# Gate rows fetched by transfers, half-chunk score products in couples of 64 rows, and three small moves in a two-layer decoder trunk

## The chip, the cores and the metric

The kernel runs on one core of a Trainium2 chip. The metric is the device time of one execution in microseconds, lower is better. Before the change it is 1235.92 us, the median of three runs (1235.68 to 1236.24). All times below are microseconds unless they are marked ns.

## The reference

Two decoder layers over 512 tokens of width 1024, in float32. Layer 0 mixes tokens with an mLSTM (4 heads of width 192, a matrix memory with input and forget gates), layer 1 with differential attention (6 pairs of heads of width 64). Both have a cross attention to 256 memory tokens and a SwiGLU block.

```python
def mlstm_mixer(h, w_in, conv_w, conv_b, gate_b, head_norm):
    p = h @ w_in
    qk_raw = p[..., :2 * MIX_WIDTH]                 # 2 * 768 columns
    gates = p[..., 4 * MIX_WIDTH:4 * MIX_WIDTH + 2 * M_HEADS] + gate_b
    qk = jax.nn.silu(causal_depthwise_conv(qk_raw, conv_w, conv_b))
    q = qk[..., :MIX_WIDTH].reshape(B, S, M_HEADS, M_HEAD_DIM)      # 4 heads of 192
    k = qk[..., MIX_WIDTH:].reshape(B, S, M_HEADS, M_HEAD_DIM) * (M_HEAD_DIM ** -0.5)
    i_pre, f_pre = gates[..., :M_HEADS], gates[..., M_HEADS:]
    hs = mlstm_chunkwise(q, k, v, i_pre, f_pre)     # scores q k^T, weighted by gate sums, causal
    ...

for i in range(DEPTH):                              # DEPTH = 2
    h = rmsnorm(x, norm1[i])
    mix, xq = mlstm_mixer(...) if i == 0 else diff_attention(...)
    xo = memory_cross_attention(xq, mem, mem_norm[i], w_mem_kv[i], xq_norm[i], xk_norm[i])
    x = x + concat([mix, xo]) @ w_out[i]
    h = rmsnorm(x, norm2[i])
    x = x + (silu(gate) * up) @ w_down[i]
```

## The kernel before, in words

Activations stand transposed: features on the partitions, the 512 tokens along the free axis, in eight tiles of 128 features. A **dense product** of a 128-wide output tile is a sum over eight input tiles `k`, and each `k` has three matmuls, because every operand is split into a rounded part and a rest (`Hh` and `Hl` for the input, `w_hi` and `w_lo` for the weight): `Hh,w_hi`, `Hl,w_hi` and `Hh,w_lo`, all of them in the fp32r type in one pass. SyncE (SP) loads one raw weight tile after another, GpSimd (POOL) splits each into `w_hi` (one instruction, L568) and `w_lo` (mostly one instruction per group of 256 columns, L573). Matmuls on plain f32 operands (`tmp,cn`, `QK`, `QK,KZ`, `rm,ones`) are run in two passes, and the trace has a record for each pass. The order of the work on each engine is written out by hand; engines wait for each other on semaphores.

**Start (0 to 140 us).** Projection tiles of layer 0 alternate with memory tiles (256 memory tokens, `Ah,w_hi` with 256 columns) and small jobs. The eight gate rows of the mixer (`i_pre`, `f_pre` for four heads) and eight lower parts of them come out of one product with 16 rows, `PS[0:16, 6]`; VectorE (DVE) scales them into `tmp[6][0:16]` (L1136, semaphore `g_free`). TensorE (PE) then adds upper and lower parts, and moves the result to partitions 0 to 3, with two selection products of 16 rows (L1658, L1659). The first sum goes to bank 6 (input gates) and is read by DVE when it forms `a_row`; the second goes to bank 3 (forget gates) and is read by ScalarE (ACT) at L699. Behind them on PE come the column sum of the memory's squares (`rm,ones`) and the first memory tile (`Ah,w_hi`).

**mLSTM scores (141 to 215 us).** A head is 192 wide, which is one full chunk of 128 features and half a chunk. Chunks 1 and 4 of q and of k (`HALF_CHUNK`) hold the halves of two heads each, in partitions 0 to 63 and 64 to 127. `head_scores(h)` forms four key blocks `s` of 128 keys; block `s` has `512 - 128 s` columns and its own bank of PSUM (`S_BANK`). Each block is two products over 128 rows: one on the full chunk, one on the half chunk, where the other head's 64 rows of k are zero. For that DVE writes zeros at L1141 and L1142 (semaphore `k_zero`), and `silu` (L657) puts the two halves of k of such a chunk in two instructions, one into `KZ`, one into `QK`. Blocks 0 and 1 wait until ACT has read the cross attention's scores from the banks (`ms_exp`), blocks 2 and 3 wait for `hout`, the two head-output instructions L1261 and L1262 of DVE. DVE weights each block when it is done (L1230, semaphore `s_done`).

**Differential attention (646 to 840 us).** Six pairs of heads, `c` = 0 to 5, are worked in turn among dense tiles. For pair `c` and query block `u`: PE forms the scores (`b_s`, matmuls named `QT_HI` and `QR_LO`), DVE masks them and takes the row maximum (`b_max`, L1453 to L1456), ACT takes exponentials (`b_exp`, L931, two activations each with a sum that is read out), DVE scales and subtracts (`b_prob`, L1465 to L1467), PE transposes (`b_t`, L1952, after ACT has emptied the bank by `b_at`, L940), and a product with V follows. The output `x` of an earlier pair is rounded meanwhile into the dense operand by ACT (`c_hi`, `Ah`, L986) and DVE (`c_lo`, `Al`, L1493), and `co_ready` tells PE.

## Time and profile before

| | us |
|---|---|
| median of three runs | 1235.92 |
| the profiled execution, its own time | 1235.87 |
| its span, first to last instruction | 1234.0 |
| PE busy | 1227.9 (99%) |
| POOL busy | 844.9 (68%) |
| DVE busy | 519.2 (42%) |
| ACT busy | 360.7 (29%) |

The profiled execution lies 1.9 us above its span, and within 0.1 us of the median. Busy time is the union of the records of an engine. [...] A record that spans several passes is marked by its count (x2, x4), and then runs from the first start to the last end.

### The profile page before, as it was taken

The numbers are of one execution on the slowest core, as the hardware profiler recorded it, in microseconds if no ns is written. First come the engines' busy times: TensorE is split into PE (matmuls) and PEld (weight loads), VectorE is DVE, ScalarE is ACT, GpSimd is POOL, SyncE is SP. The second block draws the span as 40 slices with busy tenths as digits, with TensorE's granted clock in tenths as the row PEclk, the third lists the DMA queues.
The fourth block names the chain that finished last, engine by engine and source line by source line (L and its number), as shares of the span: only waits on it lengthen the run. The fifth ranks groups of instructions, "written<-read, shape, count | busy, mean of one in ns | idle before, by whom it ended". The sixth has DMA issues, their size and how long they took to land.

```text
span 1234.0 us, 16220 instructions
## 1 busy us (share of the span) xinstructions
PE 1227.9 (99%) x5848; PEld 1002.9 (81%) x5848; DVE 519.2 (42%) x795; ACT 360.7 (29%) x716; POOL 844.9 (68%) x1029
## 2 busy tenths in 40 slices
PE   9999999999999999999999999999999999999998
PEld 7888877788888888888888777778888888888887
DVE  6954434644222233112345888884423113221331
ACT  6523456633220011001141666655322001100110
POOL 7998433567777777777776444536678777777775
PEclk9999999999999999999999999999999999999999
DMA  7234211123232222222243222222323223323223
GB/s 274 96 122 146 69 53 46 57 86 99 97 102 95 92 102 91 96 102 98 77 132 101 71 69 71 70 69 68 101 86 102 103 85 102 102 87 101 96 72 105
DMA packets 35067, 116.99 MB, mean 95 GB/s; under 512 B 4417, under 2 KB 4930, under 8 KB 34886
## 3 DMA queue, kind: packets, MB, share of 16 engines
q1 hardware_dynamic: 33416, 112.82, 27.4%
...
## 4 chain that ended last, share of the span: by engine, by line
PE 97%; DVE 1%; ACT 1%; issue 0%; DMA 0%; POOL 0%; ACTq 0%; SPq 0%; POOLq 0%
PE PS L1551 95%; PE PS L1952 1%; DVE nmB L1455 0%; DVE Al L1279 0%; PE PS L1795 0%; DMA w_raw<-in_wt_dram 0%; PE PS L1980 0%; PE PS L1921 0%; PE PS L1913 0%; PE PS L1619 0%; PE PS L1905 0%; DVE PS L1453 0%; DVE PB L1467 0%; ACT tmp L800 0%; ACT tmp L808 0%
## 5 line engine op out<-in xcount | busy, mean ns | idle before, releaser
L573 POOL TENSOR_TENSOR w_lo<-w_raw,w_hi 128x256 fp32r<-128x256 f32 (+1 forms) x800 | 617.5, 803 | 17.0
L568 POOL TENSOR_SCALAR w_hi<-w_raw 128x1024 fp32r<-128x1024 f32 (+2 forms) x204 | 214.7, 1052 | 356.8 <-PE PS L1551 356.7
L1551 PE MATMUL PS<-Hh,w_hi 128*128 128x512 f32 x1072 | 428.2, 399 | 0.0
L1551 PE MATMUL PS<-Hl,w_hi 128*128 128x512 f32 x1072 | 417.9, 390 | 0.3 <-DVE Hl L1059 0.3
L1551 PE MATMUL PS<-Hh,w_lo 128*128 128x512 f32 x1072 | 418.0, 390 | 0.0
L1551 PEld LDWEIGHTS PS<-Hh,w_hi 128*128 128x128 f32 x1072 | 201.3, 188 | 47.7 <-issue 8.1
L1551 PEld LDWEIGHTS PS<-Hh,w_lo 128*128 128x128 f32 x1072 | 201.2, 188 | 42.9
L1551 PEld LDWEIGHTS PS<-Hl,w_hi 128*128 128x128 f32 x1072 | 201.5, 188 | 40.4 <-issue 1.0
L1551 PE MATMUL PS<-Ah,w_hi 128*128 128x512 f32 (+1 forms) x544 | 207.9, 382 | 0.1
L1551 PE MATMUL PS<-Ah,w_lo 128*128 128x512 f32 (+1 forms) x544 | 205.0, 377 | 0.0
L1551 PE MATMUL PS<-Al,w_hi 128*128 128x512 f32 (+1 forms) x544 | 204.9, 377 | 0.0
L864 ACT ACTIVATE tmp<-tmp 128x512 f32<-128x512 f32 x44 | 27.9, 634 | 315.3 <-DVE tmp L1371 315.3
L1551 PEld LDWEIGHTS PS<-Ah,w_hi 128*128 128x128 f32 x544 | 102.3, 188 | 20.8 <-issue 1.5
L1551 PEld LDWEIGHTS PS<-Ah,w_lo 128*128 128x128 f32 x544 | 102.3, 188 | 19.0
L1551 PEld LDWEIGHTS PS<-Al,w_hi 128*128 128x128 f32 x544 | 102.4, 188 | 18.8 <-issue 0.5
L1373 DVE TENSOR_TENSOR tmp<-PS,rinv 128x512 f32<-128x512 f32 x44 | 30.4, 691 | 200.4 <-PE PS L1551 200.4
L866 ACT ACTIVATE Ah<-tmp 128x512 f32 x44 | 27.8, 632 | 251.7 <-DVE tmp L1376 251.7
L1371 DVE TENSOR_TENSOR tmp<-PS,rinv 128x512 f32<-128x512 f32 x44 | 30.4, 692 | 90.0 <-PE PS L1551 89.5
L1392 DVE TENSOR_TENSOR xT<-xT,PS 128x512 f32 x24 | 16.5, 688 | 105.8 <-PE PS L1551 105.8
L1334 DVE TENSOR_TENSOR xT<-xT,PS 128x512 f32<-128x512 f32 x40 | 27.4, 686 | 77.8 <-PE PS L1551 77.8
L1379 DVE TENSOR_TENSOR Al<-tmp,Ah 128x512 f32 x44 | 41.0, 931 | 40.0 <-ACT Ah L866 40.0
L1376 DVE TENSOR_TENSOR tmp<-tmp 128x512 f32<-128x512 f32 x44 | 39.3, 892 | 5.4
...
## 6 DMA issues: line engine op xcount, KB each, us to landing
...
QKR<-QKP ACTq DMA_DIRECT2D x24, 128.0 KB, 4.3
...
```

The lines of the kernel that those rows point to most:

```text
L568: nc.gpsimd.tensor_scalar(w_hi[:, sl, 0:nk], w_raw[:, raw, 0:nk], 0.0, 1.0, ALU.add, ALU.mult).then_inc(w_round, 1)
L573: lo = nc.gpsimd.tensor_tensor(w_lo[:, sl, w], w_raw[:, raw, w], w_hi[:, sl, w].bitcast(F32), ALU.subtract)
L864: nc.scalar.activation(tmp[0][:, 0:SEQ], tmp[1][:, 0:SEQ], ACT.Silu).then_inc(silu_done, 1)
L866: nc.scalar.activation(Ah[:, bass.ds(i, 1)], tmp[3][:, 0:SEQ].rearrange("p (a n) -> p a n", a=1), ACT.Copy).then_inc(f_hi, 1)
L1334: nc.vector.tensor_tensor(xT[:, k], xT[:, k], PS[:, bank], ALU.add).then_inc(dense_free, 1)
L1371: nc.vector.tensor_tensor(tmp[1][:, 0:SEQ], PS[:, base % 2], rinv[:], ALU.mult).then_inc(dense_free, 1)
L1373: nc.vector.tensor_tensor(tmp[2][:, 0:SEQ], PS[:, (base + 1) % 2], rinv[:], ALU.mult).then_inc(dense_free, 1)
L1376: nc.vector.tensor_tensor(tmp[3][:, 0:SEQ], tmp[0][:, 0:SEQ], tmp[2][:, 0:SEQ], ALU.mult).then_inc(gu_ready, 1)
L1379: nc.vector.tensor_tensor(Al[:, bass.ds(i, 1)], one, Ah[:, bass.ds(i, 1)].bitcast(F32), ALU.subtract).then_inc(f_ready, 1)
L1392: nc.vector.tensor_tensor(xk_, xk_, PS[:, b:b + 1], ALU.add).then_inc(dense_free, 1)
L1551: return nc.tensor.matmul(out_, a, b, start=start, stop=stop)
L1952: last = nc.tensor.transpose(PS[:, 2 + u % 2, k * P:(k + 1) * P], PB[:, 0, W_OFF[u] + k * P:W_OFF[u] + (k + 1) * P], ident)
```

## The change

Three parts. **Gates:** the two selection products on PE are gone. ACT issues three transfers inside SBUF, after `first_tap(0)`, which copy rows 4 to 7, 8 to 11 and 12 to 15 of `tmp[6]` to partitions 0 to 3 of `tmp[0]`, `tmp[7]` and `tmp[1]`; DVE adds upper and lower parts with two additions behind `mem_lo(0)`. **Half chunks:** `KZ` and the zeros go. SP issues eight transfers that put chunks 1 and 4 of q and k into `QSW` and `KSW` with their 64-row halves exchanged, four ahead of the load of tile `T_HEAD + 1`, four ahead of that of tile `T_HEAD + 5` (these wait for the fourth `s_done`). `head_scores` takes the key blocks two at a time: full chunk of the first, full chunk of the second, then both half chunks as products over 64 rows, the first on the head's own rows and the second on the exchanged copy, which lies in the other 64 rows of the array. **Attention:** `b_s(c, 3)` is issued one or two steps later in the dense tile, in the last pair too; `b_t(c, 1)` one step later; `c_hi` stands ahead of `b_exp(c, 2)`, `c_lo` ahead of `b_max(c, 3)`.

```diff
@@ SP, ahead of the load of tile n
+                if n in (T_HEAD + 1, T_HEAD + 5):
+                    i = (n - T_HEAD) // 4
+                    c = HALF_CHUNK[i]
+                    sp.wait_ge(qk_ready, MC + c + 1)
+                    if i:
+                        sp.wait_ge(s_done, NT)
+                    for r in (0, 64):
+                        sp.dma_start(QSW[64 - r:P - r, i], QK[r:r + 64, c]).then_inc(sw_in, 16)
+                        sp.dma_start(KSW[64 - r:P - r, i], QK[r:r + 64, MC + c]).then_inc(sw_in, 16)
                 load(n)
@@ ACT
-                if c - MC in HALF_CHUNK:
-                    act.wait_ge(k_zero, 1)
-                    nc.scalar.activation(KZ[64:P, HALF_CHUNK.index(c - MC)], y[64:P], ACT.Silu)
-                    nc.scalar.activation(QK[0:64, c], y[0:64], ACT.Silu).then_inc(qk_ready, 1)
-                else:
-                    nc.scalar.activation(QK[:, c], y, ACT.Silu).then_inc(qk_ready, 1)
+                nc.scalar.activation(QK[:, c], y, ACT.Silu).then_inc(qk_ready, 1)
...
             first_tap(0)
+            act.wait_ge(g_free, 1)
+            for row, dst in ((1, tmp[0]), (2, tmp[7]), (3, tmp[1])):
+                act.dma_start(dst[0:MH, 0:SEQ], tmp[6][row * MH:(row + 1) * MH, 0:SEQ]).then_inc(gsel_done, 16)
             act.wait_ge(mss_done, 1)
...
-            act.wait_ge(gsel_done, 1)
-            link(nc.scalar.activation(tmp[0][0:MH, 0:SEQ], PS[0:MH, 3], ACT.Identity, bias=gb[:, 1:2]))
+            act.wait_ge(g_free, 2)
+            link(nc.scalar.activation(tmp[0][0:MH, 0:SEQ], tmp[0][0:MH, 0:SEQ], ACT.Identity, bias=gb[:, 1:2]))
...
                 b_exp(c, 1)
                 if c + 1 < MC:
                     b_sq(c + 1)
-                b_exp(c, 2)
                 if x is not None:
                     c_hi(x)
+                b_exp(c, 2)
@@ DVE
-            dve.wait_ge(msum_done, 1)
-            nc.vector.memset(KZ[0:64], 0.0)
-            nc.vector.memset(QK[64:P, MC + 1:MC + 5:3], 0.0).then_inc(k_zero, 1)
             v_raw(0)
...
             mem_lo(0)
+            dve.wait_ge(gsel_done, 48)
+            nc.vector.tensor_tensor(tmp[0][0:MH, 0:SEQ], tmp[0][0:MH, 0:SEQ], tmp[1][0:MH, 0:SEQ], ALU.add).then_inc(g_free, 1)
+            nc.vector.tensor_tensor(tmp[6][0:MH, 0:SEQ], tmp[6][0:MH, 0:SEQ], tmp[7][0:MH, 0:SEQ], ALU.add).then_inc(g_free, 1)
             conv(0)
...
                 b_prob(c, 1)
-                b_max(c, 3)
                 if x is not None:
                     c_lo(x)
+                b_max(c, 3)
@@ PE
             pe.wait_ge(g_free, 1)
             pe.wait_ge(std_done, 1)
-            mm(PS[0:MH, 6], cn[0:16, C_GSEL:C_GSEL + MH], tmp[6][0:16, 0:SEQ])
-            mm(PS[0:MH, 3], cn[0:16, C_GSEL + MH:C_GSEL + 2 * MH], tmp[6][0:16, 0:SEQ]).then_inc(gsel_done, 1)
             pe.wait_ge(msum_done, 1)
...
-                for s in range(NT):
...
-                    kz = KZ[:, HALF_CHUNK.index(c)] if r else QK[:, MC + c]
-                    mm(o, kz[:, s * P:(s + 1) * P], QK[:, c, s * P:SEQ], start=False).then_inc(s_done, 1)
+                i = HALF_CHUNK.index(c)
+                pe.wait_ge(sw_in, 64 * (i + 1))
+                for s0 in (0, 2):
+                    for s in (s0, s0 + 1):
...
+                        mm(o, QK[:, MC + f, s * P:(s + 1) * P], QK[:, f, s * P:SEQ], stop=False)
+                    for s in (s0, s0 + 1):
+                        o = PS[:, S_BANK[s], s * P:SEQ]
+                        if s % 2:
+                            w, m = KSW[64 - r:P - r, i], QSW[64 - r:P - r, i]
+                        else:
+                            w, m = QK[r:r + 64, MC + c], QK[r:r + 64, c]
+                        mm(o, w[:, s * P:(s + 1) * P], m[:, s * P:SEQ], start=False).then_inc(s_done, 1)
...
-                    if k in (0, 2):
-                        b_s(c, 2 + k // 2)
-                    if k in (5, 6):
-                        b_t(c, k - 5)
+                    if k == 0:
+                        b_s(c, 2)
+                    if k == (3 if x is None else 2):
+                        b_s(c, 3)
+                    if k == 5:
+                        b_t(c, 0)
+                    if k == (7 if x is None else 6):
+                        b_t(c, 1)
...
-                    if i in (1, 2, 4):
-                        b_s(c, i - i // 4)
+                    if i in (1, 2, 5):
+                        b_s(c, i - 2 * (i // 5))
```

The lines below are rows of an engine's program in its order; a name such as `PS<-Hh,w_lo` is output and inputs, and square brackets hold the semaphores that an instruction waits on. Lines of the changed kernel have other numbers: L1560 is the matmul helper that was L1551, and L1502, L1462 to L1465 and L1474 to L1476 were L1493, L1453 to L1456 and L1465 to L1467.

On PE, at the end of the second value tile, where the gate rows are selected. Before:

```order
L1551 MATMUL PS<-Hh,w_lo 128x512
L1551 MATMUL PS<-tmp,cn 4x512 [waits std_done,g_free]
L1551 MATMUL PS<-tmp,cn 4x512
L1551 MATMUL PS<-rm,ones 128x256 [waits msum_done]
L1551 MATMUL PS<-Ah,w_hi 128x256 [waits mg_ready,dense_free,w_first]
```

After:

```order
L1560 MATMUL PS<-Hh,w_lo 128x512
L1560 MATMUL PS<-rm,ones 128x256 [waits msum_done,std_done,g_free]
L1560 MATMUL PS<-Ah,w_hi 128x256 [waits mg_ready,dense_free,w_first]
L1560 MATMUL PS<-Al,w_hi 128x256
L1560 MATMUL PS<-Ah,w_lo 128x256
```

The two selection products (16 rows in, 4 rows out, 512 columns) are gone, and nothing takes their place on PE.

On PE, the scores of head 1 (`QK,KZ` is a half chunk over 128 rows, `QSW,Ah` the exchanged copy over 64 rows). Before:

```order
L1551 MATMUL PS<-QK 128x512 [waits ms_exp,p_ready]
L1551 MATMUL PS<-QK,KZ 128x512
L1551 MATMUL PS<-QK 128x384 [waits ms_exp,p_ready]
L1551 MATMUL PS<-QK,KZ 128x384
L1551 MATMUL PS<-QK 128x256 [waits hout,p_ready]
L1551 MATMUL PS<-QK,KZ 128x256
L1551 MATMUL PS<-QK 128x128 [waits hout,p_ready]
L1551 MATMUL PS<-QK,KZ 128x128
L1551 MATMUL PS<-Hh,w_hi 128x512 [waits dense_free,w_first]
```

After:

```order
L1560 MATMUL PS<-QK 128x512 [waits ms_exp,p_ready,sw_in]
L1560 MATMUL PS<-QK 128x384 [waits ms_exp,p_ready]
L1560 MATMUL PS<-QK 128x512
L1560 MATMUL PS<-QSW,Ah 128x384
L1560 MATMUL PS<-QK 128x256 [waits hout,p_ready]
L1560 MATMUL PS<-QK 128x128 [waits hout,p_ready]
L1560 MATMUL PS<-QK 128x256
L1560 MATMUL PS<-QSW,Ah 128x128
L1560 MATMUL PS<-Hh,w_hi 128x512 [waits dense_free,w_first]
```

Eight products of 128 rows become four of 128 rows and two couples of 64 rows, and block 1's full product with its wait now stands ahead of block 0's half product.

On DVE, in pair 4 of the attention: `b_prob` of block 1 (L1465 to L1467), `b_max` of block 3 (L1453 to L1456) and `c_lo` (`Al`). Before:

```order
L1465 RECIPROCAL rsB<-rsB 128x2 [waits bexp]
L1466 TENSOR_SCALAR PB<-PB,rsB,lam 128x384 [waits vch]
L1467 SCALAR_TENSOR_TENSOR PB<-PB,rsB 128x384 [waits vch]
L1453 TENSOR_TENSOR PS<-PS,cn 128x2x128 [waits bs_done]
L1455 TENSOR_REDUCE nmB<-PS 128x2 [waits vch]
L1456 TENSOR_TENSOR nmB<-nmB,rqk_all 128x2 [waits vch]
L1493 TENSOR_TENSOR Al<-PS,Ah 128x256 [waits co_hi]
```

After:

```order
L1474 RECIPROCAL rsB<-rsB 128x2 [waits bexp]
L1475 TENSOR_SCALAR PB<-PB,rsB,lam 128x384 [waits vch]
L1476 SCALAR_TENSOR_TENSOR PB<-PB,rsB 128x384 [waits vch]
L1502 TENSOR_TENSOR Al<-PS,Ah 128x256 [waits co_hi]
L1462 TENSOR_TENSOR PS<-PS,cn 128x2x128 [waits bs_done]
L1464 TENSOR_REDUCE nmB<-PS 128x2 [waits vch]
L1465 TENSOR_TENSOR nmB<-nmB,rqk_all 128x2 [waits vch]
```

`c_lo` has moved ahead of the three instructions of `b_max` of block 3.

## Rows read from the trace of the kernel before

**Rows 1.** Page: the chain that ended last, share of the span.

```profile
PE 97%; DVE 1%; ACT 1%; issue 0%; DMA 0%; POOL 0%; ACTq 0%; SPq 0%; POOLq 0%
```

**Rows 2.** Timeline of PE at the gates: start, us, line, operation, count.

```profile
33.31 0.39 PE L1551 MATMUL PS<-Hh,w_lo 128*128 128x512 f32 x1
33.63 1.88 PE L1551 MATMUL PS<-tmp,cn 16*4 16x512 f32 x4
35.43 0.70 PE L1551 MATMUL PS<-rm,ones 128*128 128x256 f32 x2
...
36.09 0.28 PE L1551 MATMUL PS<-Al,w_hi 128*128 128x256 f32 x1
```

**Rows 3.** Timeline of DVE, 29 to 66 us.

```profile
31.07 0.91 DVE L1142 MEMSET QK<- 64x1024 f32 x1 [0.25 <-issue]
...
45.03 0.69 DVE L1106 TENSOR_TENSOR tmp<-PS,rinv 128x512 f32<-128x512 f32 x1 [0.96 <-PE PS L1551]
...
63.20 0.41 DVE L1111 TENSOR_TENSOR kv<-PS,rm 128x256 f32<-128x256 f32 x1
```

**Rows 4.** Timelines of POOL, 52 us, and of PE, 56 and 65 us.

```profile
52.40 3.15 POOL L573 TENSOR_TENSOR w_lo<-w_raw,w_hi 128x256 fp32r<-128x256 f32 x4
...
56.40 0.40 PE L1551 MATMUL PS<-Hh,w_hi 128*128 128x512 f32 x1
...
65.59 0.40 PE L1551 MATMUL PS<-Hh,w_hi 128*128 128x512 f32 x1
```

**Rows 5.** Timeline of PE, scores of head 1.

```profile
164.20 1.02 PE L1551 MATMUL PS<-QK 128*128 128x512 f32 x2
...
165.92 0.81 PE L1551 MATMUL PS<-QK 128*128 128x384 f32 x2
...
167.21 0.59 PE L1551 MATMUL PS<-QK 128*128 128x256 f32 x2
...
168.08 0.38 PE L1551 MATMUL PS<-QK 128*128 128x128 f32 x2
```

**Rows 6.** Timeline of PE, products over 64 rows among dense ones.

```profile
159.08 0.40 PE L1551 MATMUL PS<-Hh,w_lo 128*128 128x512 f32 x1
159.41 1.13 PE L1551 MATMUL PS<-xk,xqA 64*128 64x256 f32 x8
...
160.81 0.39 PE L1551 MATMUL PS<-Hl,w_hi 128*128 128x512 f32 x1
161.04 0.39 PE L1551 MATMUL PS<-Hh,w_lo 128*128 128x512 f32 x1
```

**Rows 7.** Timeline of DVE beside head 1's scores.

```profile
165.61 0.73 DVE L1262 TENSOR_SCALAR QK<-PS,gcol 64x512 f32<-64x512 f32 x1
```

**Rows 8.** DMA issues: KB each, median us to landing.

```profile
QKR<-QKP ACTq DMA_DIRECT2D x24, 128.0 KB, 4.3
```

**Rows 9.** Timeline of PE at the attention's waits, pairs 0, 4 and 5.

```profile
682.93 0.33 PE L1551 MATMUL PS<-QT_HI 64*128 64x128 f32 x2 [0.50 <-ACT PB L931]
...
688.69 0.41 PE L1952 MATMUL PS<-cn,PB 128*128 128x128 f32 x2
...
805.16 0.40 PE L1551 MATMUL PS<-Hh,w_lo 128*128 128x512 f32 x1
806.20 0.52 PE L1952 MATMUL PS<-cn,PB 128*128 128x128 f32 x3 [0.65 <-DVE Al L1493]
...
807.96 0.38 PE L1952 MATMUL PS<-cn,PB 128*128 128x128 f32 x2
...
828.53 0.39 PE L1551 MATMUL PS<-Ah,w_lo 128*128 128x512 f32 x1
829.06 0.33 PE L1551 MATMUL PS<-QT_HI 64*128 64x128 f32 x2
```

**Rows 10.** Timelines of DVE and ACT, pair 4.

```profile
805.64 0.42 DVE L1493 TENSOR_TENSOR Al<-PS,Ah 128x256 fp32r<-128x256 f32 x1
...
806.64 0.98 ACT L940 ACTIVATE ATB<-PS 128x512 f32<-128x512 f32 x2
```

More of the change, by code:

```diff
@@ L216, in hybrid_trunk @@
         V = sb("V", [P, NT, MH * VW], scope=sA)
-        KZ = sb("KZ", [P, 2, SEQ], scope=sA)
+        QSW = sb("QSW", [P, 2, SEQ], scope=sA)
+        KSW = Ah[:, 0:2].bitcast(F32)
         Mrow = sb("Mrow", [MH, SEQ], scope=sA)
@@ L329, in hybrid_trunk @@
         v_ones = sem("v_ones")
-        k_zero = sem("k_zero")
+        sw_in = sem("sw_in")
         m_rows = nc.dram_tensor("m_rows", (MH, SEQ), F32).ap()
@@ L1166, in _ @@
             link(nc.vector.scalar_tensor_tensor(L, F, 0.0, L, ALU.min, ALU.subtract))
+            dve.wait_ge(g_free, 3)
             link(nc.vector.memset(tmp[7][0:MH, 0:SEQ], 1.0))
@@ L1169, in _ @@
             link(nc.vector.tensor_tensor_scan(b_row, tmp[7][0:MH, 0:SEQ], L, 0.0, ALU.mult, ALU.add))
-            link(nc.vector.scalar_tensor_tensor(a_row, PS[0:MH, 6], gb[:, 0:1], b_row, ALU.add, ALU.subtract))
+            link(nc.vector.scalar_tensor_tensor(a_row, a_row, gb[:, 0:1], b_row, ALU.add, ALU.subtract))
             link(nc.vector.tensor_tensor_scan(Mrow[:], a_row, a_row, 0.0, ALU.max, ALU.max))
@@ L1713, in head_scores @@
                     pe.wait_ge(kn_ready, 2)
-                for s in range(NT):
-                    o = PS[:, S_BANK[s], s * P:SEQ]
-                    if h >= 1:
-                        pe.wait_ge(p_ready, NT * (h - 1) + s + 1)
-                    if h >= 1 and s >= 2:
-                        pe.wait_ge(hout, 2 * h)
-                    elif h >= 1:
-                        pe.wait_ge(ms_exp, 4 * h if s else 4 * h - 2)
-                    if h == 0 and s == NT - 1:
-                        pe.wait_ge(qk_ready, QKC)
-                    mm(o, QK[:, MC + f, s * P:(s + 1) * P], QK[:, f, s * P:SEQ], stop=False)
-                    kz = KZ[:, HALF_CHUNK.index(c)] if r else QK[:, MC + c]
-                    mm(o, kz[:, s * P:(s + 1) * P], QK[:, c, s * P:SEQ], start=False).then_inc(s_done, 1)
+                i = HALF_CHUNK.index(c)
[3 more added lines that the diff above has]
+                        o = PS[:, S_BANK[s], s * P:SEQ]
+                        if h >= 1:
+                            pe.wait_ge(p_ready, NT * (h - 1) + s + 1)
+                        if h >= 1 and s >= 2:
+                            pe.wait_ge(hout, 2 * h)
+                        elif h >= 1:
+                            pe.wait_ge(ms_exp, 4 * h if s else 4 * h - 2)
+                        if h == 0 and s == NT - 1:
+                            pe.wait_ge(qk_ready, QKC)
+                        mm(o, QK[:, MC + f, s * P:(s + 1) * P], QK[:, f, s * P:SEQ], stop=False)
+                    for s in (s0, s0 + 1):
+                        o = PS[:, S_BANK[s], s * P:SEQ]
+                        if s % 2:
[3 more added lines that the diff above has]
+                        mm(o, w[:, s * P:(s + 1) * P], m[:, s * P:SEQ], start=False).then_inc(s_done, 1)
             def head_pv(h):
```

2 lines of the change are left out of this document (1 added, 1 removed).

## The prediction

> **What bounds the kernel now.** I first read the table of the page: PE is busy for 1227.9 of the span's 1234.0 us, and the chain that ended last is PE's own work for 97% [rows 1]. The clock was granted in full throughout. So time goes or comes in two ways only: columns that PE no longer streams (or drains that it makes), and idle gaps of PE. Then I read PE's timeline at the three places of the change, and the timelines of DVE, ACT and POOL beside them, for what is late once PE is early. A change of another engine's work is worth nothing here unless it closes a gap of PE.
>
> **Gates.** Before, the last product of the second value tile starts at 33.31 and the second product of the memory tile at 36.09 [rows 2], 2.78 us apart. After the change three things are left between those starts: the dense product's 0.23 (the step from 160.81 to 161.04 [rows 6]), the memory's column sum in two passes of 256 columns (two such plain products over 128 rows take 0.87 from 167.21 to 168.08 [rows 5], so 0.43), and half a dense step for `Ah,w_hi`, 0.12. That is 0.78. The saving is **2.00 us**: four passes of 512 columns at 0.43 (from 164.20 to 165.92 four passes take 1.72 [rows 5]) are 1.72, and the other 0.28 is drain and exposed weight load on both sides of the 16-row products.
>
> This is kept only if nothing else is late by then. Three covers:
> - DVE loses two fills of 0.91 [rows 3], and its short waits beside them, about 2.1 in all, so `mem_lo(0)` can end about 34.5. ACT issues its transfers from about 30.0 to 31.5 (three, at an estimated 0.5 each). The nearest transfer inside SBUF lands after 4.3 [rows 8]; this one is a sixteenth in size, at a busier time, so I take the same: 35.8. DVE stands at the wait of the two additions, 1.3 us, and everything behind them with it: `conv(0)`, `v_raw(1)`, `mem_out(0)`. The additions are 4 x 512, an estimated 0.7 each (DVE takes 0.69 for 512 columns over 128 partitions [rows 3]). So `conv(0)` starts at about 37, where it started before (36.9): DVE gains nothing there. It had 0.96 of idle time for PE at 45.03 [rows 3]; that goes, so later work comes about 0.9 earlier. The tightest need behind it is `mem_out(2)`, which ends at 63.61 [rows 3] with PE wanting the tile from 65.59 [rows 4]: 2.0 before, 62.7 against 63.59 after. 0.9 us are left.
> - POOL: `w_lo` of tile 9 has its second part by about 54.1 (L573, four from 52.40, 0.8 each; tile 9 waits for the first two) and PE starts the tile at 56.40 [rows 4]: 2.3 of slack for 2.00 of advance. POOL itself waited for PE a few us ahead of that, and follows it. 0.3 to 0.7 are left.
> - Later, POOL waits for PE, not the other way round, and keeps doing so.
> Taken: -2.00. If the covers fail in part, up to 2.0 comes back, so this term lies between -2.0 and 0.
>
> **Couples.** A head before: 3.88 from 164.20 to 168.08 and two products of 128 columns, 0.22 each [rows 5]: 4.32. Columns after: the four full products 0.86, 0.65, 0.43, 0.22, and two couples as long as their wider member, 0.86 and 0.43: 3.45. So 0.87 less, if the members of a couple run beside each other. That they do: eight passes of 256 columns over 64 rows come as one row of 1.13 us, last end included [rows 6]; one after the other they would need 1.72.
>
> But a couple has its price. From 159.08 to 160.81 are 1.73 us [rows 6]. The content is one dense step, 0.23, eight passes in four steps of 0.215, 0.86, and one dense step, 0.23: 1.32. **0.41** is for going into the 64-row form and out of it. Each head now does that twice, in the middle (before block 2's full product) and at the end: 0.82. Left are 0.05 a head, with the rounding of the rows up to 0.08; four heads: **-0.2**. The Trainium skill says the same in principle: "TensorEngine Tiling", Tiling Modes, Key Properties, has the engine drain on a change of tiling mode. Its table under Overview, Theoretical Speedup, gives up to 2x for a small dimension up to 64; by that alone, with free changes, the part would be worth 4 x 0.87 = 3.5. The bounds are therefore -3.5 (changes cost nothing) and, with members one after the other, 4 x 0.82 = +3.3.
>
> Waits around it: block 1's full product comes 0.86 earlier than before, block 2's 0.36 earlier (166.85 instead of 167.21 [rows 5]); `hout` is given at 165.61 + 0.73 = 166.34 [rows 7], so 0.5 is left. DVE gets block 0 at 166.8 instead of 165.9, when it has only just ended its output instructions; block 1 comes as before. The product with V is over 1 us behind. The eight transfers cost SP two stops of up to 2 us ahead of weight loads which POOL needs some 25 us later; they take none of PE's time. The zeros and the second `silu` are off the path (counted above).
>
> **Attention.** PE's gaps there, each the start in the row less the start ahead less 0.23: pair 0, before the scores of block 3, 0.50 by the row's own count; pair 4, 806.20 - 805.16 - 0.23 = 0.82, waiting for `Al`; pair 5, 829.06 - 828.53 - 0.23 = 0.30, some 0.1 of it the way into the 64-row form, 0.2 a wait [rows 9].
> - Pair 0: the scores go one step later, so the 0.5 goes. But DVE works there without a gap, and the bank copy that the transposes of 688.69 [rows 9] need hangs on DVE's chain; it doesn't come earlier, PE comes there as late as before. 0.
> - Pairs 1 to 3 show no gap; the copy gets about 0.34 later (DVE's 0.42 for `Al` stands ahead of it), with 0.5 spare. 0.
> - Pair 4: `Al` (805.64 [rows 10]) no longer waits behind `b_max`'s three instructions, 1.0 us; the 0.82 goes. In return `b_max(3)`, `b_exp(3)` and the copy (806.64 [rows 10], first half 0.6) come 0.33 later: 807.56, and with 0.15 to get to PE its transposes start at 807.7, against 807.96 before [rows 9]. -0.27.
> - Pair 5: one step later, the wait of 0.2 goes and nothing behind it is tight. -0.21.
> Together **-0.5**; bounds: 0 (all given back), -1.5 (0.5 + 0.8 + 0.2, nothing given back).
>
> **The sum** against the profiled execution: 1235.87 - 2.0 - 0.2 - 0.5 = 1233.17. The median is 0.05 above that execution: 1233.2.
>
> **Rivals.** What a measurement can tell here is 0.2%, 2.5 us: faster begins at 1233.45.
> - A, slower: couples in series. If the second member of a couple waits for the first (unlike the equal members of rows 6 these differ in width), the content stays 4.32 a head and the four changes of form add 0.82: +3.3 instead of -0.2. The sum is +0.8: 1236.7, slower than before. It decides from 0.63 us of loss a head, which eats the other 2.5. Against it: [rows 6]. Chance 0.06, and in half of that the gates' saving is lost too (C), which gives up to 1238.7, beyond the 0.2% at 1238.4.
> - B, changes of form nearly free, or only one of the two dear, or the pair gaps not given back: the couples give -1.5 to -3.5 and the sum is -4 to -6: with -2.0, 1231.4. For it: 0.41 was measured between a dense product and plain ones, and part of it may belong to the change of number format, which the couples in a head don't make. Against it: the timeline shows no gap of that kind between a head's last plain product and the dense ones behind it. At its end, with all 3.5, it is 1229.9. The Trainium skill's "up to 2x" ("TensorEngine Tiling", Theoretical Speedup) is that end. Chance 0.10.
> - C, the gates' gain comes back in the next 30 us: the transfers land 2 us later than I take (no row shows a transfer inside SBUF in this busy stretch), then DVE is 1.1 us too late at `mem_out(2)`, or POOL doesn't follow: -1.6 or less in all, 1234.3. For it: margins of 0.9 and 0.3 to 0.7. Chance 0.22.
> - D, the attention's terms come to nothing or turn, or the couples cost a few tenths more a head (0.1 more each is +0.4): 1233.6 to 1234.2. Chance 0.17.
> - My forecast, 1232.6 to 1233.6: 0.45.
>
> **Range and chances.** From the cases: the range 1231.8 to 1234.5 leaves out A (0.06), the far half of B (0.05) and the worse third of C (0.08). Faster by over 0.2%: the forecast's part below 1233.45, 0.42, and B, 0.10, so 0.52; slower by over 0.2%: half of A, 0.03; within 0.2%: the rest, 0.45.
>
> **What would show it.** Right, if PE's start of the memory tile's second product is at 34.09, and no new gap of PE stands before 70 us; if DVE shows one stop of about 1.3 us behind `mem_lo(0)`; if each head takes 4.24 to 4.27 from its first product to the dense one behind, and the couple's two products start within some ns of each other; if the gaps at 682.9, 806.2 and 829.1 (less 2 us) are gone, that at 688.7 has grown by half a microsecond. Wrong, if a couple's second member begins when the first ends (A), if a head takes under 4.0 (B), if PE waits for DVE or POOL between 40 and 66 us (C), or if the transposes of pairs 1 to 3 wait for ACT (D).

## The result, and the profile after

The changed kernel takes 1237.92 us (median of 20 runs, 1235.84 to 1242.19), the kernel before 1235.99 on the same chip (20 runs, 1235.66 to 1236.63). The ratio is 1.002, 95% interval 1.0014 to 1.0026: slower by about 2 us where 2.7 less were forecast. Four executions far outside all others (1651.85 of `pair0_both` at a mean granted clock of 0.697; of the kernel before 1358.53 at 0.851, 3285.66 and 4381.93 at 1.000) are left out of the ranges and counts in this document.

The 20 runs are two groups, told apart by their mean granted clock: eight with 1.000, 1235.84 to 1237.00, their median 1236.1, and twelve with 0.996 to 0.999, 1237.68 to 1242.19. All 20 of before have 1.000. So there are two things to find: why nothing is gained at full clock, and why the clock falls in 12 of 20. The profiled execution took 1239.10, span 1237.3.

A dense product's row of 0.39 to 0.40 runs past the start of the next one, 0.23 later. So what a product costs PE is read from start to start, and a gap below is a step less 0.23.

The waits of PE (us in total, times, longest), 5.0 in all against 2.4 before. The third row, 1.0 at the start of the kernel, stands in both:

```profile
PE PS L1560 <- DVE kv L1119: 2.0, 2, 1.0
PE PS L1967 <- DVE PB L1476: 1.3, 1, 1.3
PE PS L1560 <- POOL hpi L545: 1.0, 1, 1.0
PE PS L1967 <- ACT ATB L948: 0.4, 1, 0.4
PE PS L1560 <- DVE Al L1079: 0.3, 1, 0.3
```

`kv` is `mem_out`, `PB` is `b_prob`. **Gates.** The timelines of PE (first three rows, against [rows 2]; then tiles 9 and 11, against [rows 4]) and of DVE (against [rows 3]):

```profile
33.67 0.39 PE L1560 MATMUL PS<-Hh,w_lo 128*128 128x512 f32 x1
33.90 0.59 PE L1560 MATMUL PS<-rm,ones 128*128 128x256 f32 x2
34.45 0.28 PE L1560 MATMUL PS<-Al,w_hi 128*128 128x256 f32 x1
...
56.70 0.47 PE L1560 MATMUL PS<-Hh,w_hi 128*128 128x512 f32 x1 [1.05 <-DVE kv L1119]
...
67.12 0.47 PE L1560 MATMUL PS<-Hh,w_hi 128*128 128x512 f32 x1 [0.98 <-DVE kv L1119]
```

```profile
31.77 5.65 DVE L1079 SCALAR_TENSOR_TENSOR Al<-mT,gcol,Ah 128x256 fp32r<-128x256 f32 x8
37.34 1.21 DVE L1158 TENSOR_TENSOR tmp<-tmp 4x512 f32<-4x512 f32 x1
38.48 1.22 DVE L1159 TENSOR_TENSOR tmp<-tmp 4x512 f32<-4x512 f32 x1
...
48.09 1.62 DVE L1174 SCALAR_TENSOR_TENSOR tmp<-tmp 4x512 f32<-4x512 f32 x1
...
66.56 0.41 DVE L1119 TENSOR_TENSOR kv<-PS,rm 128x256 f32<-128x256 f32 x1
```

The same of DVE, and POOL beside it, in the kernel before:

```profile
33.63 3.24 DVE L1071 SCALAR_TENSOR_TENSOR Al<-mT,gcol,Ah 128x256 fp32r<-128x256 f32 x8
...
46.08 0.67 DVE L1166 SCALAR_TENSOR_TENSOR tmp<-tmp 4x512 f32<-4x512 f32 x1
...
33.86 3.94 POOL L568 TENSOR_SCALAR w_hi<-w_raw 128x1024 fp32r<-128x1024 f32 x1 [1.40 <-PE PS L1551]
```

And POOL in the changed kernel:

```profile
29.92 3.10 POOL L583 TENSOR_TENSOR w_lo<-w_raw,w_hi 128x256 fp32r<-128x256 f32 x4
34.23 1.17 POOL L578 TENSOR_SCALAR w_hi<-w_raw 128x1024 fp32r<-128x1024 f32 x1 [1.21 <-PE PS L1560]
35.48 3.68 POOL L583 TENSOR_TENSOR w_lo<-w_raw,w_hi 128x256 fp32r<-128x256 f32 x4
```

From 33.67 to 34.45 are 0.78, where 2.78 were: the 2.00 are saved, exactly. But DVE has not gained anything. It starts the memory's lower parts at 31.77, 1.9 earlier than before, and needs 5.65 for the eight where it needed 3.24. Three of the eight start while POOL stands idle and take 0.47 each; the five that meet an instruction of POOL take 0.65 to 1.26. The additions take 1.2 each and not 0.7, and another instruction of the gate rows with two inputs in SBUF (L1174, L1166 before) takes 1.62 instead of 0.67. There is no idle stretch ahead of the first addition, so the transfers were not late (ACT's queue issued them at 27.2 to 28.6). `mem_out(2)` starts at 66.56 instead of 63.20, and against the same steps of the kernel before PE loses 1.3 and 1.2 at the two tiles and 0.7 at the first memory tile: 3.2 in all.

**Couples.** PE's timeline of head 1, against [rows 5]:

```profile
165.70 2.29 PE L1560 MATMUL PS<-QK 128*128 128x512 f32 x5
167.31 0.91 PE L1560 MATMUL PS<-QSW,Ah 64*128 64x384 f32 x2
167.83 1.85 PE L1560 MATMUL PS<-QK 64*128 64x512 f32 x6
...
170.16 0.40 PE L1560 MATMUL PS<-Hl,w_hi 128*128 128x512 f32 x1
```

From 165.70 to 170.16 less a dense step, 0.23, are 4.23; 4.24 to 4.27 were forecast, and 4.32 it was. So the members of a couple do run beside each other: one after the other they would have made a head about 5.1 long.

**Attention.** Timelines of PE (against [rows 9]), DVE and POOL at pair 0, after and before, and the busy time by window (columns: us, then PE, PEld, DVE, ACT, POOL busy with their counts, PE's granted clock, DMA share, GB/s):

```profile
688.97 0.40 PE L1560 MATMUL PS<-Hh,w_lo 128*128 128x512 f32 x1
690.69 0.44 PE L1967 MATMUL PS<-cn,PB 128*128 128x128 f32 x2 [1.33 <-DVE PB L1476]
690.97 0.51 PE L1560 MATMUL PS<-cn,QS 128*128 128x2 f32 x4
```

```profile
688.48 1.21 DVE L1475 TENSOR_SCALAR PB<-PB,rsB,lam 128x256 f32<-128x256 f32 x1
689.73 0.91 DVE L1476 SCALAR_TENSOR_TENSOR PB<-PB,rsB 128x256 f32<-128x256 f32 x1
...
688.50 1.05 POOL L578 TENSOR_SCALAR w_hi<-w_raw 128x1024 fp32r<-128x1024 f32 x1 [4.19 <-PE PS L1560]
689.63 3.03 POOL L583 TENSOR_TENSOR w_lo<-w_raw,w_hi 128x256 fp32r<-128x256 f32 x4
```

Before:

```profile
687.14 0.41 DVE L1466 TENSOR_SCALAR PB<-PB,rsB,lam 128x256 f32<-128x256 f32 x1
687.59 0.49 DVE L1467 SCALAR_TENSOR_TENSOR PB<-PB,rsB 128x256 f32<-128x256 f32 x1
...
688.07 1.05 POOL L568 TENSOR_SCALAR w_hi<-w_raw 128x1024 fp32r<-128x1024 f32 x1 [5.09 <-PE PS L1551]
```

After, by window:

```profile
692.00:694.00 2.00, 2.00 (x13) 1.81 (x13) 2.00 (x5) 0.28 (x1) 0.66 (x1) 0.80 0.23 33
694.00:695.00 1.00, 1.00 (x5) 0.99 (x5) 1.00 (x2) 0.10 (x1) 0.00 (x0) 0.50 0.88 344
695.00:696.00 1.00, 1.00 (x4) 0.72 (x3) 0.97 (x2) 0.98 (x2) 0.00 (x0) 0.50 0.29 115
696.00:697.00 1.00, 1.00 (x5) 0.82 (x4) 0.56 (x1) 0.99 (x3) 0.00 (x0) 0.69 0.00 0
```

The gap ahead of block 2's transposes was 0.26 and is 690.69 - 688.97 - 0.23 = 1.5. POOL's split starts within 20 ns of DVE's `b_prob(2)`, and the two instructions of `b_prob(2)` take 1.21 and 0.91 (the second meets the `w_lo` of 689.63) where they took 0.41 and 0.49. Some 2.5 us behind the gap the granted clock goes to the lower of its two levels (0.50 of full, 1.2 GHz instead of 2.4) for 3.4 us. A dense step is 0.43 there and not 0.23, and PE loses 1.6.

**Theory.** An instruction of DVE with two inputs in SBUF, or with its one input and its output there, and an instruction of POOL stand in each other's way: the one that starts later waits for the one that is running. PE's advance moves POOL's next split, since POOL waits for PE, and the split falls on another instruction of DVE. The gap that this makes in pair 0 lets the clock fall. **Rivals:** the additions alone; late transfers; changes of form, or the gate part's gaps, as what lets the clock fall; DVE late in pair 0 for another reason.

### The profile page after: what moved, and what is told of

Read it like the earlier page. It is cut to its first block, busy times and chain, and to the rows that moved or that the text cites. A ratio compares the mean times of both kernels' runs of the same rounds, so it can differ in the third digit from the quotient of the medians.

```text
span 1237.3 us, 16222 instructions
## 1 busy us (share of the span) xinstructions
PE 1228.9 (99%) x5844; PEld 1002.8 (81%) x5844; DVE 524.3 (42%) x795; ACT 359.4 (29%) x714; POOL 841.9 (68%) x1029
## 4 chain that ended last, share of the span: by engine, by line
PE 93%; DVE 5%; issue 1%; ACT 1%; POOL 0%; DVEq 0%; ACTq 0%; POOLq 0%
PE PS L1560 91%; DVE Al L1079 1%; PE PS L1967 0%; DVE PB L1476 0%; DVE PS L1139 0%; DVE PB L1475 0%; DVE nmB L1464 0%; DVE tmp L1114 0%; DVE Al L1288 0%; PE PS L1810 0%; PE PS L1995 0%; PE PS L1936 0%; DVE rinv L1103 0%; PE PS L1928 0%; PE PS L1920 0%
## 5 line engine op out<-in xcount | busy, mean ns | idle before, releaser
L1560 PE MATMUL PS<-Hh,w_hi 128*128 128x512 f32 x1072 | 428.9, 400 | 2.0 <-DVE kv L1119 2.0
L1560 PE MATMUL PS<-Hh,w_lo 128*128 128x512 f32 x1072 | 418.2, 390 | 0.0
L1560 PE MATMUL PS<-Hl,w_hi 128*128 128x512 f32 x1072 | 418.1, 390 | 0.0
L1560 PEld LDWEIGHTS PS<-Hh,w_hi 128*128 128x128 f32 x1072 | 201.6, 188 | 51.6 <-issue 10.7
L1560 PEld LDWEIGHTS PS<-Hh,w_lo 128*128 128x128 f32 x1072 | 201.5, 188 | 43.0
L1560 PEld LDWEIGHTS PS<-Hl,w_hi 128*128 128x128 f32 x1072 | 201.8, 188 | 39.4 <-issue 1.0
L1560 PE MATMUL PS<-Ah,w_hi 128*128 128x512 f32 (+1 forms) x544 | 208.1, 383 | 0.3 <-DVE Al L1079 0.3
L1560 PE MATMUL PS<-Al,w_hi 128*128 128x512 f32 (+1 forms) x544 | 205.0, 377 | 0.0
L1560 PE MATMUL PS<-Ah,w_lo 128*128 128x512 f32 (+1 forms) x544 | 204.9, 377 | 0.0
L1560 PEld LDWEIGHTS PS<-Ah,w_hi 128*128 128x128 f32 x544 | 102.3, 188 | 21.7 <-issue 1.5
L1560 PEld LDWEIGHTS PS<-Ah,w_lo 128*128 128x128 f32 x544 | 102.3, 188 | 18.9
L1560 PEld LDWEIGHTS PS<-Al,w_hi 128*128 128x128 f32 x544 | 102.4, 188 | 18.7 <-issue 0.5
```

The lines of the kernel that those rows point to most:

```text
L1560: return nc.tensor.matmul(out_, a, b, start=start, stop=stop)
```

## The experiments

All were timed in 8 to 12 runs beside runs of before on the same chip (1235.97, 1236.17, 1236.03 and 1236.05 in the four groups). "Low" counts the runs with a mean granted clock under 1.000. The median of `pair0_both` is that of all 12 executions; it is 1238.11 without the one that is left out. Where kernels of two groups are compared below, up to 0.2 of the difference can be that of the chips, as the medians of before show.

| label | median, us | runs | low | ratio, interval |
|---|---|---|---|---|
| gates_only | 1236.48 | 1236.23 to 1236.82 | 0 of 11 | 1.0004, 0.9995 to 1.0013 |
| couples_only | 1235.79 | 1235.14 to 1235.95 | 0 of 11 | 0.9997, 0.9988 to 1.0006 |
| attention_only | 1239.30 | 1236.33 to 1241.56 | 8 of 11 | 1.0025, 1.0016 to 1.0034 |
| couples_adjacent | 1234.06 | 1233.67 to 1234.52 | 0 of 11 | 0.9984, 0.9975 to 0.9993 |
| gates_and_couples | 1236.16 | 1235.71 to 1237.21 | 0 of 11 | 1.0000, 0.9991 to 1.0009 |
| gates_dve_moved | 1234.76 | 1234.33 to 1235.46 | 0 of 11 | 0.9990, 0.9981 to 0.9999 |
| attention_without_pair0 | 1235.58 | 1235.17 to 1237.21 | 3 of 11 | 0.9999, 0.9990 to 1.0008 |
| attention_pool_held | 1235.69 | 1235.43 to 1237.18 | 2 of 11 | 0.9997, 0.9988 to 1.0006 |
| gates_sums_in_psum | 1235.59 | 1235.05 to 1236.44 | 0 of 11 | 0.9996, 0.9987 to 1.0005 |
| units_order_only | 1235.88 | 1235.40 to 1237.52 | 2 of 11 | 1.0000, 0.9991 to 1.0009 |
| pair0_scores_only | 1236.44 | 1235.96 to 1238.00 | 4 of 11 | 1.0007, 0.9998 to 1.0016 |
| pair0_turn_only | 1235.79 | 1235.59 to 1236.23 | 0 of 11 | 0.9999, 0.9990 to 1.0007 |
| pair0_both | 1238.34 | 1236.47 to 1240.19 | 6 of 11 | 1.0019, 1.0010 to 1.0028 |
| changed_pool_held | 1235.48 | 1234.90 to 1238.25 | 2 of 11 | 0.9998, 0.9989 to 1.0007 |
| best_plain_attention | 1232.87 | 1232.52 to 1233.86 | 0 of 10 | 0.9975, 0.9966 to 0.9985 |
| best_moved_attention | 1232.85 | 1232.38 to 1233.96 | 1 of 8 | 0.9976, 0.9965 to 0.9986 |

### One part at a time

`gates_only`, `couples_only`, `attention_only` and `gates_and_couples` are the kernel before with those hunks of the diff alone.

> Only the gate part is made (selection products gone, three transfers, two additions); the zeros of the half chunks stay on DVE. Theory 1 (DVE's instructions that read and write SBUF and POOL's split instructions slow each other): PE's step over the gate place is 2.0 us shorter; the memory's lower parts start where they started before, so POOL's w_hi again stands back for them (about 4 us) and they take 0.4 each; only the two additions come on top, 1.3 to 2.4 us, on a margin of 2.0 + 0.96 for 2.0 of advance: PE's gaps ahead of tiles 9 and 11 are 0.4 to 1.5 us in all, and the time is 0.5 to 1.6 us below before. Theory 2 (the additions alone are the cost, whatever stands where): the gaps are as in the changed kernel, 2.3 us, and the time is 0.3 us above before. Theory 3 (the transfers land late): DVE shows an idle stretch in front of the first addition.

DVE's timeline:

```profile
33.84 3.24 DVE L1074 SCALAR_TENSOR_TENSOR Al<-mT,gcol,Ah 128x256 fp32r<-128x256 f32 x8
37.01 1.52 DVE L1156 TENSOR_TENSOR tmp<-tmp 4x512 f32<-4x512 f32 x1
38.46 1.22 DVE L1157 TENSOR_TENSOR tmp<-tmp 4x512 f32<-4x512 f32 x1
...
51.10 1.35 DVE L1177 SCALAR_TENSOR_TENSOR tmp<-tmp,gb 4x512 f32<-4x512 f32 x1
```

With the zeros still there, the lower parts start where they used to and take 3.24 again: the 5.65 come from their new place. That much is as theory 1 has it; its size is not. The additions cost 2.7, `a_row` 1.35 where it took 0.74, and PE loses 0.6 and 1.3 at the two tiles and 0.6 at the first memory tile: the time is 0.5 above before and not 0.5 to 1.6 below. In the time this is nearer to theory 2, which had 0.3 above: in this kernel most of the loss is the additions'. Theory 3 falls, DVE does not wait ahead of the additions.

> Only the couples (with the eight transfers, without the zeros and the second silu). If the sum of the prediction holds, each head takes 4.24 us to the dense product behind it, against 4.32, and the time is 0.3 us below before, with the clock granted in full in all executions. Rival: the changes of form among the heads are what lets the granted clock fall in the changed kernel's executions; then some executions here are 1 to 6 us longer too. DVE is 2.1 us earlier ahead of the memory's lower parts, so those collide with POOL's w_lo here (0.7 each instead of 0.4); without the additions and with PE late, as before, no gap of PE follows.

1235.79 against 1235.97: 0.2 less, the clock full in all; the interval reaches past 1, so it rests on the trace, in which each head takes 4.24 and PE ends the fourth one 0.4 earlier than before. The changes of form don't lower the clock. The memory's lower parts take 5.64 here, from 31.74, with no change at the gates: it is the missing zeros that move them onto POOL's instructions, and by itself it costs PE nothing.

> Only the moves in the attention stage. Theory 1: in pair 0, PE reaches the dense tile's end sooner, POOL's next split starts some 0.9 us sooner and falls on DVE's two instructions for block 2, which take 1.2 and 0.9 instead of 0.41 and 0.49; the transposes of block 2 wait about 1.5 us instead of 0.26, and the granted clock falls to a half a few us behind that in part of the executions: time 0 to +0.5 us in executions at full clock, +1 to +6 in the others, median about +1 to +2. Rival: the gap of 1.5 us is due to the shift that the rest of the change brings, or the fallen clock to the gaps of the gate part; then this kernel is 0.2 to 0.5 below before with a steady time.

Gap 1.50, three runs at full clock with 1236.33 to 1236.45 (0.4 above before), eight with 1237.89 to 1241.56. The attention part alone makes the long runs, and the median 3.3 over before.

> The changed kernel without the moves in the attention stage. Theory: the gaps of PE ahead of tiles 9 and 11 stand as in the changed kernel, 1.2 and 1.1 us, because the memory's lower parts start 2.1 us sooner and so fall on POOL's w_lo instructions (5.6 us instead of 3.2), and the two additions take 1.2 each; the clock is granted in full in all executions, since the gap of 1.5 us in pair 0 is not there. Time 1235.5 to 1235.9, steady. Rival: the gate part's two gaps of over 1 us let the clock fall; then some executions are 1 us and more above the rest.

The losses at the gates are those of the changed kernel (1.3, 1.2 and 0.7), and there is no low run: gaps of that size between the dense products of 56 and 66 us leave the clock alone. 1235.5 to 1235.9 were expected; 1236.16 came, the same as before.

### What makes DVE late at the gates

```diff
@@ gates_dve_moved, DVE
-            mem_out(1)
             conv(2)
             q_out(3)
-            mem_lo(1)
             mem_out(2)
             q_out(4)
             conv(3)
             mem_out(3)
+            mem_lo(1)
...
             link(nc.vector.memset(tmp[7][0:MH, 0:SEQ], 1.0))
+            mem_out(1)
             dve.wait_ge(vT_done, 2)
```

> As gates_only, with two of DVE's jobs in another order: the multiplication that frees the bank for tile 9 (mem_out of the second memory tile) goes ahead of the two scans, and the memory's lower parts of the second layer (7.3 us, needed some 40 us later) go behind mem_out of the fourth memory tile. If PE only waits there because DVE is late, the gaps of 0.5 and 1.3 us ahead of tiles 9 and 11 go, and the time is 1.3 to 1.8 us below gates_only, 0.9 to 1.3 below before. If POOL is as late as DVE by then, 0.3 to 0.7 us of gap stay, with POOL as the one waited for.

1234.76, 1.7 below `gates_only` and 1.4 below before; both gaps are gone. Of the gate part's 2.0, 1.4 are kept once two jobs of DVE stand elsewhere. PE waits for POOL at neither tile. So DVE being late was all that stood in the way there.

```diff
@@ gates_sums_in_psum, DVE (ACT and a_row read PS[0:MH, 3] and PS[0:MH, 6])
-            nc.vector.tensor_tensor(tmp[0][0:MH, 0:SEQ], tmp[0][0:MH, 0:SEQ], tmp[1][0:MH, 0:SEQ], ALU.add)
-            nc.vector.tensor_tensor(tmp[6][0:MH, 0:SEQ], tmp[6][0:MH, 0:SEQ], tmp[7][0:MH, 0:SEQ], ALU.add)
+            nc.vector.tensor_tensor(PS[0:MH, 3], tmp[0][0:MH, 0:SEQ], tmp[1][0:MH, 0:SEQ], ALU.add)
+            nc.vector.tensor_tensor(PS[0:MH, 6], tmp[6][0:MH, 0:SEQ], tmp[7][0:MH, 0:SEQ], ALU.add)
```

> As gates_only, but the two additions write to PSUM (the banks where the products on PE put the same rows), and ACT and DVE read them there, as before the change. Nothing else differs. Theory (an instruction of DVE that touches PSUM is not slowed by POOL's splits, one with SBUF on both sides is): the additions take 0.7 each instead of 1.5 and 1.2, a_row 0.74 instead of 1.35, DVE is 1.9 us earlier at mem_out of the third memory tile; PE's gaps ahead of tiles 9 and 11 shrink from 0.5 and 1.3 to 0.0 to 0.3, and the time is 1.2 to 1.6 us below gates_only. Rival (4 rows of 512 cost 1.2 us wherever they stand, or reading SBUF isn't what is slow): same time as gates_only.

```profile
37.27 1.53 DVE L1156 TENSOR_TENSOR PS<-tmp 4x512 f32<-4x512 f32 x1
38.72 1.22 DVE L1157 TENSOR_TENSOR PS<-tmp 4x512 f32<-4x512 f32 x1
...
51.36 0.74 DVE L1177 SCALAR_TENSOR_TENSOR tmp<-PS,gb,tmp 4x512 f32<-4x512 f32 x1
```

Half of the expectation failed. The additions write to PSUM and are as slow as before; `a_row`, which now reads one of its two inputs from PSUM, takes 0.74 again. So it is two inputs out of SBUF that meet POOL, not the output. The rival, that 4 rows of 512 cost 1.2 wherever they stand, fails on the trace before: an instruction of that shape with two inputs in SBUF took 0.67 there (46.08) and 1.62 in the changed kernel. The time is 0.9 below `gates_only`, not 1.2 to 1.6. The Trainium skill has this rule ("SBUF — State Buffer", section "SBUF: two separate sides"): a pair of ports is shared by DVE and GpSimd, whichever starts first has it for its whole instruction, and DVE needs it with two SBUF inputs or in its two-port mode. The trace agrees in kind: in the changed kernel the 128x256 instruction took 1.21 beside a split of 1.05 that began in the same 20 ns, against 0.41 by itself. That is 0.25 less than the split and the instruction one behind the other.

### Pair 0

```diff
@@ attention_without_pair0 (the other attention moves stay)
-                    if k == (3 if x is None else 2):
+                    if k == 2:
                         b_s(c, 3)
...
-                    if k == (7 if x is None else 6):
+                    if k == 6:
                         b_t(c, 1)
@@ attention_pool_held and changed_pool_held, POOL, ahead of a tile's w_hi
+                if n == bv_tile(0) + 2:
+                    pool.wait_ge(ba_ready, 3)
```

> As attention_only, but pair 0 keeps its scores of block 3 and its transposes of block 1 at their old steps. Theory: the gap of pair 0 is 0.57 and 0.25 again, the clock is granted in full in all executions, pairs 4 and 5 give 0.2 each: 1235.5, steady. Rival (the moves of c_hi and c_lo or the last pair are what spoils it): the median stays above 1237.

Steady but for three runs at clock 0.999, 1237.1 to 1237.2. Without pair 0 the long runs of 1239 to 1241 are gone, and the rival with them. The 3 of 11 weren't expected.

> As attention_only in full, with one wait more: POOL holds the split of one weight tile in pair 0 until DVE has done b_prob of block 2 (about 1 us, POOL is over 4 us ahead there). Theory (the gap of 1.5 us comes from POOL's split and DVE's two instructions slowing each other): they take 0.41 and 0.49 again, the gap is 0.83, the clock stays at full, and the time is 1235.6 to 1235.8. Rival (DVE is late for another reason): gap, clock and time stay as in attention_only.

Gap 0.83 and `b_prob(2)` at 0.41 and 0.48, as reckoned, by a wait that takes work from nobody: DVE was late because of POOL's split. 1235.69, as expected; but the clock doesn't stay at full, there are two low runs (1236.87, 1237.18).

The three kernels on pair 0 alone are before with `b_s(0, 3)` at step 3 instead of 2 (`scores`), `b_t(0, 1)` at step 7 instead of 6 (`turn`), or both.

> Of the whole change only this: in pair 0 the scores of block 3 go one step later. PE's gap of 0.57 goes, PE ends the tile 0.57 sooner, and POOL's split starts 0.57 sooner, 0.1 before DVE's b_prob of block 2 ends its first instruction; the second one (0.49 before) should be slowed to about 0.9, the first barely. The gap ahead of block 2's transposes becomes 0.83 + 0.4 = 1.2, the time at full clock 0.4 above before, and in part of the executions the clock falls, in fewer than in attention_only or for shorter. If DVE is not hit, the gap is 0.83 and the time equals before.

> Of the whole change only this: in pair 0 the transposes of block 1 go one step later, behind the tile's last dense product. The tile ends 0.24 sooner for POOL, which starts at 687.8 instead of 688.07: the second instruction of b_prob of block 2 is hit for its last 0.2 at most. Gaps as before, 0.57 and 0.3 to 0.5, clock at full in all executions, time within 0.2 of before.

> Both moves of pair 0, nothing else. If pair 0 alone makes the long executions, this has the gap of 1.5, 0.65 above before at full clock (1236.7), and the clock falls in about half of the executions or more, which then are 2 to 5 us longer, as in attention_only.

Timelines of POOL and DVE in pair 0, `pair0_turn_only`, then `pair0_scores_only`, then `pair0_both`:

```profile
687.69 1.22 POOL L568 TENSOR_SCALAR w_hi<-w_raw 128x1024 fp32r<-128x1024 f32 x1 [4.79 <-PE PS L1551]
...
687.07 0.41 DVE L1466 TENSOR_SCALAR PB<-PB,rsB,lam 128x256 f32<-128x256 f32 x1
687.52 0.48 DVE L1467 SCALAR_TENSOR_TENSOR PB<-PB,rsB 128x256 f32<-128x256 f32 x1
```

```profile
687.55 1.04 POOL L568 TENSOR_SCALAR w_hi<-w_raw 128x1024 fp32r<-128x1024 f32 x1 [4.53 <-PE PS L1551]
...
687.19 0.41 DVE L1466 TENSOR_SCALAR PB<-PB,rsB,lam 128x256 f32<-128x256 f32 x1
687.64 1.23 DVE L1467 SCALAR_TENSOR_TENSOR PB<-PB,rsB 128x256 f32<-128x256 f32 x1
```

```profile
687.08 1.05 POOL L568 TENSOR_SCALAR w_hi<-w_raw 128x1024 fp32r<-128x1024 f32 x1 [4.19 <-PE PS L1551]
...
687.05 1.22 DVE L1466 TENSOR_SCALAR PB<-PB,rsB,lam 128x256 f32<-128x256 f32 x1
688.30 0.91 DVE L1467 SCALAR_TENSOR_TENSOR PB<-PB,rsB 128x256 f32<-128x256 f32 x1
```

This is the plainest reading of the study. Where DVE's second instruction starts first (687.52), it takes 0.48 and POOL's takes 1.22 instead of 1.05; where POOL is 90 ns ahead of it (687.55), it takes 1.23; where POOL comes 0.5 earlier still, both are hit, the second one by the `w_lo` behind the split. (In that last kernel DVE's record starts 30 ns ahead of POOL's, and yet it is DVE that waits: so close together the records don't tell who was first.) The gaps are 0.23, 1.02 and 1.50, the low runs 0, 4 and 6 of 11, and these lie at 1237.5 to 1238.0 for the middle gap and 1238.1 to 1240.2 for the largest. At full clock the three medians are 1235.79, 1236.33 and 1236.78 against 1236.05.

> The whole change, with POOL's one split in pair 0 held until b_prob of block 2 is done. The account of the result: at full clock the changed kernel's 1236.1 less 0.65, 1235.5; the long executions go but for some 1 us longer ones that pair 4's gap makes (2 or 3 of 11). Median 1235.4 to 1235.8, 2 us below the changed kernel. If the clock also falls for another reason in the changed kernel, the median stays above 1237.

The whole change with that one wait: 1235.48, 2.4 below the changed kernel, as expected. Two runs of 11 stay low (1236.91, 1238.25). The profiled execution, 1236.71 at full clock, is 1.2 above the median of the eleven.

```diff
@@ units_order_only, ACT and DVE, nothing else
-                b_exp(c, 2)
                 if x is not None:
                     c_hi(x)
+                b_exp(c, 2)
...
-                b_max(c, 3)
                 if x is not None:
                     c_lo(x)
+                b_max(c, 3)
```

> Only c_hi ahead of b_exp(2) and c_lo ahead of b_max(3), no step of PE moved. Pair 4's gap of 0.82 at the transposes of block 1 goes, one of 0.55 at those of block 2 comes, which stand right ahead of the stretch of transposes and narrow products in front of the next tile: 0.25 us below before at full clock, 1235.7. If the fallen clock in 3 of 11 executions of attention_without_pair0 comes from this gap's new place, some executions here are 1 to 2 us longer as well; if it comes from the last pair's scores one step later, none is.

As expected in kind: pair 4's gap of 0.82 at 806.20 goes and one of 0.61 comes at the transposes of block 2, so that PE gains 0.1 to 0.2 and not 0.25, and 2 of 11 runs are at 0.999 (1237.11, 1237.52). So these low runs come with the new order of the units and don't need the last pair's move. The median, 1235.88 against 1236.03, can't be told from before.

### Better versions

```diff
@@ couples_adjacent, PE (full(s), half(s): the two products of block s; wait(s): its waits)
+                for s in (0, 1):
+                    wait(s)
+                    full(s)
+                for s in (0, 1):
+                    half(s).then_inc(s_done, 1)
+                for s in (2, 3):
+                    wait(s)
+                for s in (2, 3):
+                    half(s)
+                for s in (2, 3):
+                    full(s).then_inc(s_done, 1)
```

> As couples_only, with the two couples of a head made side by side (full 0, full 1, couple 0 and 1, couple 2 and 3, full 2, full 3), so that a head changes form twice and not four times. If each way in or out costs 0.2 us, a head takes 3.83 to 3.85 us and the kernel is 1.6 us below couples_only, 1.9 below before. If the cost stands per couple and not per change of form, it equals couples_only.

```profile
163.93 2.29 PE L1553 MATMUL PS<-QK 128*128 128x512 f32 x5
165.53 0.91 PE L1553 MATMUL PS<-QSW,Ah 64*128 64x384 f32 x2
166.06 0.59 PE L1553 MATMUL PS<-QK 64*128 64x512 f32 x1
166.28 0.38 PE L1553 MATMUL PS<-QSW,Ah 64*128 64x128 f32 x2
...
168.00 0.39 PE L1553 MATMUL PS<-Hl,w_hi 128*128 128x512 f32 x1
```

From 163.93 to 168.00 less 0.23: 3.84, where four changes of form gave 4.23. The price stands per change of form, 0.2 each, and the kernel is 1.9 faster than before, its interval clear of 1.

`best_plain_attention` is `gates_and_couples` with the edits of `gates_dve_moved`, `gates_sums_in_psum` and `couples_adjacent`; `best_moved_attention` adds the attention moves except pair 0's.

> Gates with DVE's two jobs moved and the sums in PSUM, couples side by side, the attention stage as before the change. Sum of the single effects against before: -1.4 (gates_dve_moved), -1.9 (couples_adjacent), less up to 0.4 for the memory's lower parts, which start sooner without the zeros and fall on POOL's w_lo: -2.9 to -3.5, 1232.5 to 1233.1, at full clock in all executions.

> As best_plain_attention, with the attention moves except pair 0's: another 0.4 less in executions at full clock, and in some executions 1 to 2 us more, as in attention_without_pair0; median 1232.2 to 1233.0. If the fallen clock needs what the rest of the change did before it, none of the executions has it.

Both are 3.2 us below before, within what was expected, and can't be told apart: of the further 0.4 at full clock 0.1 shows. The one without the attention moves is the one to keep: no low run, against one of 8 (1233.96).

## Why the prediction was wrong

The measured 1237.92 lies among the numbers of rival A, but A's mechanism, couples in series, did not come: a head takes 4.23. That the number fits is chance.

- **Gates, the saving (-2.00):** right on PE, 2.00 measured.
- **Gates, the cover on DVE:** this step failed. The prediction took `mem_lo(0)` "about 34.5" from 3.24 us at the old place, and the additions at "an estimated 0.7 each" from an instruction that reads PSUM. In their new places these instructions read SBUF twice beside POOL's splits: 5.65 and 1.2 each. `conv(0)`, forecast at 37, starts at 39.63, and the 0.9 us that was to be left became losses of 1.3, 1.2 and 0.7 on PE. The tile of the first of them, 9, had been looked at for POOL only. The 3.24 was low because POOL's split had stood back: in the trace before its one `w_hi` at 33.86 took 3.94. The case C was listed, with a chance of 0.22, but with the wrong mechanism (late transfers, which were not late) and too small a price. The POOL margin, also thought tight, never mattered: POOL follows PE.
- **Couples (-0.2):** right in the working, 4.23 a head; that is -0.4 for the four on PE, -0.2 in the medians of `couples_only`.
- **Attention, pair 0 (0):** this step failed too. "PE comes there as late as before" held DVE's chain fixed. PE was earlier in the tile, so POOL's split was 0.9 earlier, and `b_prob(2)` was hit: the gap grew by 1.24 and not by the half microsecond that gives the advance back. 0.7 net (`pair0_both` at full clock, 1236.78 against 1236.05).
- **Pair 4 (-0.27) and pair 5 (-0.21):** right, -0.2 each on PE in `attention_without_pair0`. The median of its eight runs at full clock is 1235.5 against 1236.17 of before on the same chip.
- **The clock:** not in the prediction at all. "The clock was granted in full throughout" was read as a property of the kernel. It costs the median 1.8 (1237.92 against 1236.1 at full clock).
- The sum of what PE's steps in the profiled execution show against before, without the fallen clock: -2.0 gates, +3.2 behind them, -0.4 couples, +0.7 pair 0, -0.5 pairs 4 and 5: +1.0. The eight runs at full clock are only 0.1 above before. Profiled executions differ by up to 0.5 in their first ten us (the products on `ones` stand 0.21 apart until 4.1 us in the trace before and until 7.1 in the changed kernel's, 0.11 after that), and the profiled one of `changed_pool_held` is 1.2 above its median, so a profile need not be typical; what makes up this residue of 0.9 is open.

What stays open: where the clock falls in the low runs of `units_order_only` and `attention_without_pair0`; none of their profiled executions was low. That it is pair 4's new gap is the likeliest reading, not shown. And only one low execution has a profile, the changed kernel's at 0.999. A mean of 0.996, which five of its runs have, makes some 10 us at the lower level in all (an estimate: 0.004 of 1240, by 0.5); where these lie isn't shown. That the gap in pair 0 is what brings them rests on the counts: 8 and 6 of 11 with the gap of 1.50, 0 of 11 in `pair0_turn_only` with 0.23, and 2 of 11 instead of 12 of 20 once POOL's split is held in the whole change.
